# Transition matrices of a WKV scan: two heads worked half a level apart, projection products in pairs, VectorE's other work cut into pieces

## The reference

```python
def step(state, inp):
    r_t, w_t, k_t, v_t, a_t, b_t = inp
    sa = jnp.einsum('bhij,bhj->bhi', state, a_t)
    state = state * w_t[:, :, None, :] + sa[..., None] * b_t[:, :, None, :] + v_t[..., None] * k_t[:, :, None, :]
    return state, jnp.einsum('bhij,bhj->bhi', state, r_t)
```

## Time and profile before

| | |
|---|---|
| Time, median of 3 runs | 2726.47 us (2725.36 to 2730.03) |
| Time of the profiled execution | 2733.0 us |
| Span of the profiled execution | 2731.2 us |
| TensorE busy | 2640.0 us, 97% of the span |
| VectorE busy | 1676.8 us, 61% |
| ScalarE, GpSimd busy | 693.8 us, 25%; 317.5 us, 12% |
| Mean granted TensorE clock | 0.989 |

### The profile page before, as it was taken

One profiled execution on the slowest core, in us unless ns is written; L12 is line 12 of the kernel. 1 busy time (PEld: TensorE's weight loads), 2 busy tenths in 40 slices (PEclk: granted clock), 3 DMA queues, 4 the chain that ended last, 5 costly groups with the idle time before them and its releaser, 6 DMA issues.

```text
span 2731.2 us, 43464 instructions
## 1 busy us (share of the span) xinstructions
PE 2640.0 (97%) x17855; PEld 1986.6 (73%) x17855; DVE 1676.8 (61%) x2220; ACT 693.8 (25%) x1205; POOL 317.5 (12%) x277
## 2 busy tenths in 40 slices
PE   7999899999999999999999999989999999999998
PEld 3555456888878878888767777766677887788887
DVE  4888776555457665554476677754554665655554
ACT  4233433111010021110143344434420212201102
POOL 2000231000000010000123333332020100100001
PEclk8999899999999999999999999999999999999999
DMA  7575302333323323333311211113143333233332
GB/s 265 182 252 193 96 24 86 98 93 97 97 83 99 94 85 93 101 96 93 111 46 35 61 43 35 35 58 89 33 114 84 94 116 101 70 100 94 99 95 74
DMA packets 394851, 260.38 MB, mean 95 GB/s; under 512 B 19831, under 2 KB 376784, under 8 KB 394320
## 3 DMA queue, kind: packets, MB, share of 16 engines
q1 hardware_dynamic: 391456, 246.78, 30.4%
q0 software_dynamic: 2768, 9.83, 1.1%
q10 hardware_dynamic: 480, 1.64, 0.2%
HBM read 252.96 MB, written 4.46 MB: 94 GB/s over the span
## 4 chain that ended last, share of the span: by engine, by line
PE 87%; DVE 8%; ACT 2%; issue 2%; DMA 1%; SPq 0%; DVEq 0%; ACTq 0%
PE PS L902 13%; PE PS L904 13%; PE PS L903 13%; PE PS L1726 3%; PE PS L917 3%; PE PS L919 3%; PE PS L918 3%; PE PS L1728 2%; PE PS L1727 2%; DVE ARENA L2831 2%; PE PS L2062 2%; PE PS L2064 2%; PE PS L2063 2%; PE PS L1848 1%; PE PS L889 1%
## 5 line engine op out<-in xcount | busy, mean ns | idle before, releaser
L928 DVE CAST WH<-W 128x1024 fp32r<-128x1024 f32 x272 | 191.1, 703 | 353.6 <-PE PS L904 302.9
L930 DVE TENSOR_TENSOR WL<-W,WH 128x1024 fp32r<-128x1024 f32 x272 | 335.4, 1233 | 9.3
L903 PE MATMUL PS<-XNL,WH 128*128 128x512 f32 x832 | 323.7, 389 | 0.0
L902 PE MATMUL PS<-HH,WH 128*128 128x512 f32 x672 | 262.0, 390 | 0.2 <-DVE HL L3216 0.2
L904 PE MATMUL PS<-HH,WL 128*128 128x512 f32 x672 | 261.5, 389 | 0.0
L903 PE MATMUL PS<-HL,WH 128*128 128x512 f32 x672 | 261.4, 389 | 0.0
L902 PE MATMUL PS<-XNH,WH 128*128 128x512 f32 x512 | 199.3, 389 | 0.0
L904 PE MATMUL PS<-XNH,WL 128*128 128x512 f32 x512 | 199.2, 389 | 0.0
L903 PEld LDWEIGHTS PS<-XNL,WH 128*128 128x128 f32 x832 | 156.2, 188 | 33.0 <-issue 0.7
L917 PE MATMUL PS<-XNH,WH 128*128 128x512 f32 x384 | 151.1, 394 | 0.6 <-DVE XNL L848 0.5
L919 PE MATMUL PS<-XNH,WL 128*128 128x512 f32 x384 | 149.5, 389 | 0.0
(11 more groups left out here) (565 smaller groups left out, 5209.1 us busy)
## 6 DMA issues: line engine op xcount, KB each, us to landing
ARENA<-in_ada_w SPq DMA_DIRECT2D x80, 512.0 KB, 5.1
W<-in_ffn_w SPq DMA_DIRECT2D x64, 512.0 KB, 3.9
W<-in_w_in SPq DMA_DIRECT2D x51, 512.0 KB, 3.8
W<-in_ffn_w_gate SPq DMA_DIRECT2D x44, 512.0 KB, 3.7
W<-in_ffn_w_up SPq DMA_DIRECT2D x44, 512.0 KB, 3.6
W<-in_ffn_w_down SPq DMA_DIRECT2D x32, 512.0 KB, 3.7
W<-in_sc_w_in SPq DMA_DIRECT2D x24, 512.0 KB, 3.7
ARENA<-in_ada_w SPq DMA_DIRECT2D x8, 1024.0 KB, 18.0
```

The source lines that it names most:

```text
L902: nc.tensor.matmul(dst, WH[:, h, c], hi(k), start=(start and k == 0), stop=False)
L903: nc.tensor.matmul(dst, WH[:, h, c], lo(k), start=False, stop=False)
L928: nc.vector.tensor_copy(WH[:, h, 0:n], W[:, s, 0:n]).then_inc(parted, 1)
L930: nc.vector.tensor_tensor(WL[:, h, 0:n], W[:, s, 0:n], WH[:, h, 0:n], ALU.subtract).then_inc(freed[s], 1)
```

## The change: what it does

The two heads of a pair are no longer worked together in a step. TensorE's order in a level is now `p` of head 0, `xz` of head 1 *of the level before*, `xz` of head 0, `p` of head 1, and then one fill of two pieces of the projection in place of two lone fills. The fills begin behind level 2 and end in level 16 (in the last pass level 4 to level 32). The bonus product and head 1's `xz` of level 32 stand at the end, and `w` waits for each head's sum separately. ScalarE copies the projection's result (`raw1`) between the two heads' `pm` of level 2. VectorE's work for the next pair is cut into pieces, one behind each head's sum, and the reciprocal of 512 columns is done in three parts (176, 168, 168) in place of two. No product, sum or copy is added or dropped apart from that one reciprocal.

```diff
+        beside = {(0, 0): "d1", (0, 1): "m1 kkr", (1, 0): "d0", (1, 1): "m0", (2, 1): "nmax", (3, 0): "ninv0", (3, 1): "ninv1", (4, 0): "ninv", (4, 1): "nk"}
...
-                           + " ".join(f"p{l}0 p{l}1" + (next_pair("kss") if l == 2 else " bonus " if l == 4 else " ") + f"xz{l}0 xz{l}1"
-                                      for l in levels)
+                           + " ".join(f"p{l}0 " + (f"xz{l - 1}1 " if l else "") + f"xz{l}0" + next_pair("kss" if l == 2 else "") + f"p{l}1" for l in levels)
+                           + f" bonus xz{len(LEVELS) - 1}1 "
...
+                def masked(l, e):
+
+                    pe.wait_ge(p_pool.sem, p_pool.done(f"m{l}{e}", at))
+                    pe.wait_ge(p_dve.sem, p_dve.done(f"z{l - 1}{e}" if l else "xi", at))
+                    for t in range(NT):
+                        n = 4 * e + t
+                        for c, own in enumerate(halves):
+                            far = halves[1 - c]
+                            mm = nc.tensor.matmul(bank[e][own, t * CHUNK:(t + 1) * CHUNK], MT[far, n, :], XZ[far, e, 0, t, :], start=True, stop=True)
+                            if l == 1:
+                                mm = nc.tensor.matmul(bank[6][own, n * HEAD:(n + 1) * HEAD], GR[own, n, 2, :], TOK[own, t, 3, halves[e]], start=True, stop=True)
+                    mm.then_inc(p_pe.sem, p_pe.step(f"p{l}{e}"))
+
+                def both_sides(l, e):
+
+                    pe.wait_ge(p_act.sem, p_act.done(f"pm{l}{e}", at))
+                    pe.wait_ge(p_dve.sem, p_dve.done(f"z{l - 1}{e}" if l else "zi", at))
+                    for t in range(NT):
+                        n, cols = 4 * e + t, slice(t * CHUNK, (t + 1) * CHUNK)
+                        for c, own in enumerate(halves):
+                            if l < len(LEVELS) - 1:
+                                nc.tensor.matmul(bank[2 + 2 * e][halves[1 - c], cols], XZ[own, e, 1, t, :], PM[own, n, :], start=True, stop=True)
+                        for own in halves:
+                            mm = nc.tensor.matmul(bank[3 + 2 * e][own, cols], PM[own, n, :], XZ[own, e, 1, t, :], start=True, stop=True)
+                    mm.then_inc(p_pe.sem, p_pe.step(f"xz{l}{e}"))
+
                 for l in levels:
-                    for e in range(2):
-                        pe.wait_ge(p_pool.sem, p_pool.done(f"m{l}{e}", at))
-                        pe.wait_ge(p_dve.sem, p_dve.done(f"z{l - 1}{e}" if l else "xi", at))
-                        for t in range(NT):
-                            n = 4 * e + t
-                            for c, own in enumerate(halves):
-                                far = halves[1 - c]
-                                mm = nc.tensor.matmul(bank[e][own, t * CHUNK:(t + 1) * CHUNK], MT[far, n, :], XZ[far, e, 0, t, :], start=True, stop=True)
-                                if l == 1:
-                                    mm = nc.tensor.matmul(bank[6][own, n * HEAD:(n + 1) * HEAD], GR[own, n, 2, :], TOK[own, t, 3, halves[e]], start=True, stop=True)
-                        mm.then_inc(p_pe.sem, p_pe.step(f"p{l}{e}"))
-                    if l == 0 and ahead:
+                    masked(l, 0)
+                    if l:
+                        both_sides(l - 1, 1)
+                    elif ahead:
                         projection(1, range(5, KD), "raw0", "B", "lk")
-                    if l:
-                        early(range(2 * l - 2, 2 * l - 1))
+                    both_sides(l, 0)
                     if l == 2 and ahead:
                         pe.wait_ge(p_act.sem, p_act.done("ksq", at))
                         nc.tensor.matmul(bank[6], PAIR_ONES, YS, start=True, stop=True).then_inc(p_pe.sem, p_pe.step("kss"))
-                    if l == 4:
-                        pe.wait_ge(p_act.sem, p_act.done("kroot" if ahead else "akv", at))
-                        pe.wait_ge(p_dve.sem, p_dve.done("rk", at))
-                        nc.tensor.matmul(bank[6], PAIR_ONES, RK, start=True, stop=True).then_inc(p_pe.sem, p_pe.step("bonus"))
-                    for e in range(2):
-                        pe.wait_ge(p_act.sem, p_act.done(f"pm{l}{e}", at))
-                        pe.wait_ge(p_dve.sem, p_dve.done(f"z{l - 1}{e}" if l else "zi", at))
-                        for t in range(NT):
-                            n, cols = 4 * e + t, slice(t * CHUNK, (t + 1) * CHUNK)
-                            for c, own in enumerate(halves):
-                                if l < len(LEVELS) - 1:
-                                    nc.tensor.matmul(bank[2 + 2 * e][halves[1 - c], cols], XZ[own, e, 1, t, :], PM[own, n, :], start=True, stop=True)
-                            for own in halves:
-                                mm = nc.tensor.matmul(bank[3 + 2 * e][own, cols], PM[own, n, :], XZ[own, e, 1, t, :], start=True, stop=True)
-                        mm.then_inc(p_pe.sem, p_pe.step(f"xz{l}{e}"))
-                    if l:
-                        early(range(2 * l - 1, 2 * l))
+                    masked(l, 1)
+                    first = 2 * l if ahead else 2 * l - 2
+                    if 0 <= first < KD:
+                        early(range(first, first + 2))
+                pe.wait_ge(p_act.sem, p_act.done("kroot" if ahead else "akv", at))
+                pe.wait_ge(p_dve.sem, p_dve.done("rk", at))
+                nc.tensor.matmul(bank[6], PAIR_ONES, RK, start=True, stop=True).then_inc(p_pe.sem, p_pe.step("bonus"))
+                both_sides(len(LEVELS) - 1, 1)
                 pe.wait_ge(p_act.sem, p_act.done("akv", at))
-                pe.wait_ge(p_dve.sem, p_dve.done(f"z{len(LEVELS) - 1}1", at))
                 for n, (e, t) in enumerate(items):
+                    if t == 0:
+                        pe.wait_ge(p_dve.sem, p_dve.done(f"z{len(LEVELS) - 1}{e}", at))
...
+                        if l == 0 and e == 0 and ahead:
+                            raw("rw", 1, i, 7, p_act)
                     if l == 0 and ahead:
-                        raw("rw", 1, i, 7, p_act)
...
-            def key_norm_begun(at, p_act, p_dve):
+            def key_bound(at, p_act, p_dve):
 
                 dve.wait_ge(p_act.sem, p_act.done("kroot", at))
                 ts(RSTD[:, 0:T], ROOT[:, 0:T], 1e-12, None, ALU.max).then_inc(p_dve.sem, p_dve.step("nmax"))
-                dve.wait_ge(p_dve.sem, p_dve.done("nmax", at))
-                nc.vector.reciprocal(RSTD[:, 0:T // 2], RSTD[:, 0:T // 2]).then_inc(p_dve.sem, p_dve.step("ninv0"))
-
-            def key_norm(at, p_act, p_dve):
-
-                nc.vector.reciprocal(RSTD[:, T // 2:T], RSTD[:, T // 2:T]).then_inc(p_dve.sem, p_dve.step("ninv"))
+
+            def key_inverse(n, at, p_dve):
+
+                third = slice((0, 176, 344)[n], (176, 344, T)[n])
+                if n == 0:
+                    dve.wait_ge(p_dve.sem, p_dve.done("nmax", at))
+                nc.vector.reciprocal(RSTD[:, third], RSTD[:, third]).then_inc(p_dve.sem, p_dve.step(("ninv0", "ninv1", "ninv")[n]))
+
+            def key_normed(at, p_dve):
...
+            def beside_sums(l, e, pair, at, p_act, p_dve, signalled):
+
+                if (l, e) == (0, 0):
+                    if signalled:
+                        dve.wait_ge(go_dve.sem, signalled("out"))
+                    shifted(1, at, p_act, p_dve)
+                elif (l, e) == (0, 1):
+                    mixed_in(1, pair, at, p_dve)
+                    key_scaled(pair, at, p_dve)
+                elif (l, e) == (1, 0):
+                    shifted(0, at, p_act, p_dve)
+                elif (l, e) == (1, 1):
+                    mixed_in(0, pair, at, p_dve)
+                elif (l, e) == (2, 1):
+                    key_bound(at, p_act, p_dve)
+                elif (l, e) in ((3, 0), (3, 1), (4, 0)):
+                    key_inverse(2 * l + e - 6, at, p_dve)
+                elif (l, e) == (4, 1):
+                    key_normed(at, p_dve)
...
-                    if l == 0 and ahead:
-                        if ended:
-                            dve.wait_ge(go_dve.sem, signalled("out"))
-                        shift_mix(1, pair + 1, at, p_act, p_dve)
-                        key_scaled(pair + 1, at, p_dve)
-                    if l == 1 and ahead:
-                        shift_mix(0, pair + 1, at, p_act, p_dve)
-                    if l == 2 and ahead:
-                        key_norm_begun(at, p_act, p_dve)
-                    if l == 3 and ahead:
-                        key_norm(at, p_act, p_dve)
+                        if ahead:
+                            beside_sums(l, e, pair + 1, at, p_act, p_dve, signalled if ended else None)
                 if ahead:
```

More of the change, by code:

```diff
@@ L579, in two_blocks @@
         rf_pool = prog("rf_pool", "l1")
-        rf_dve = prog("rf_dve", "lr lk lv d0 m0 d1 m1 kkr cs t km d2 m2 nmax ninv0 ninv nk bb rt at0 at bt kt")
+        rf_dve = prog("rf_dve", "lr lk lv d0 m0 d1 m1 kkr cs t km d2 m2 nmax ninv0 ninv1 ninv nk bb rt at0 at bt kt")
```

(22 more changed lines are left out.)

## The result

The changed kernel takes 2737.09 us (median of 9 runs, 2734.87 to 2747.15); the kernel before, run beside it, 2728.31 (9 runs, 2724.7 to 2732.61). The ratio is 1.0036, with a 95% interval of 1.0025 to 1.0047: slower by 8.8 us. The forecast had 2732 and +5.6.

A forecast was written before the change was run, and what follows sets the result against it. TensorE was taken to bound the kernel, with one short wait a pass to win. Six steady passes +3.2, first +0.4, last +2.0 gave +5.6 us, 2732 on the median; range 2720 to 2738, the forecast's own 2728 to 2736.

The forecast's parts named there:

- 3.2+0.4+2.0: Extra us in all passes: six steady passes +3.2, the first about +0.4, the last +2.0; total +5.6.
- rival 3: Slower: more idle in each pass lowers TensorE's clock; 1.5 us a pass, +10.5 on the forecast, 2742; chance 0.08.
- The starting point: Whole run: forecast added +5.6 to the profiled execution's 2733.0, then took 6.5 off for the median: 2732.1, rounded to 2732.
- the 0.2 taken off for borders between small products: Four borders in levels 2 and 8: bounds 0 and 0.44 us, 0.2 taken, bringing a steady pass from +0.73 to +0.5.
- The chain of 1.69 us: One head's `xz`, sum, next `p`: 1.69 us, seen in level 2; makes head 1's `p` wait 0.59 in three levels.
- Rival 1: Faster: the wait at head 1's `p` is mostly hidden, 2717.6, or about 2725 half hidden; chance 0.18.
- Level 4: Steady pass, level 4, with 0.61 for `p`: 4.50 us against 4.11, +0.39.
- Level 8: Steady pass, level 8: key-norm product covers head 1's wait, 4.77 us against 4.81, -0.04.
- Six steady passes: The six steady passes were priced alike at +0.5 us each, +3.2 together.
- The last pass: No key-norm product, so levels 4, 8 and 16 all pay: +2.25 us, less borders +2.0.
- VectorE's pieces at nothing: VectorE's pieces behind each sum: bounds 0 and 0.3 us a pass, taken 0; tight place `m1` and `kkr` after level 2.
- the low clock stays: Last pass: 1.48 us of the old levels' time put down to low clock, expected to stay, leaving +2.25 before borders.

The follow-up runs named there:

- the double fill at level 8: lone-fill kernel with level 8's two fill pieces joined at the level's end, except in the last pass: 2723.73 us, ratio 0.9979; again 2723.79, 0.9983.
- the blocks: Changed kernel with VectorE's work for the next pair back in blocks behind a level's second sum: 2755.68 us, ratio 1.0085 to the kernel before.
- the double-fill run: Kernel before, heads still together, with both fill pieces behind `p` in levels 4 to 32 and none behind `xz`: 2747.76 us, ratio 1.0062.
- lone-fill kernel: Changed kernel with fill pieces apart again, one back between the two `xz`: 2723.57 us, ratio 0.9983 to the kernel before.

## Why the prediction was right and where it was off

- **The step that failed: all that lies outside the passes, and the granted clock over the whole run, was put at nothing.** The sum was 3.2+0.4+2.0 from the passes alone, and rival 3 priced a lower clock in the passes only. The passes gave +5.9 for +5.6, but the medians gave 8.8 and, the second time, 6.4. The three profiles of each kernel have +2.2 behind the passes and -0.9 ahead of them. Behind the passes the code is the same, and its time goes with the clock. Four profiles, all 3770 products from the end of the last pass to the end: the kernel before (first and third profile), the double fill at level 8 (second profile), and the blocks:

```profile
1864.22:2731.20 866.98, 839.97 (x3770) 667.12 (x3770) 484.46 (x609) 177.37 (x334) 60.35 (x38) 1.00 0.31 90
1856.92:2727.10 870.18, 843.83 (x3770) 670.08 (x3770) 483.35 (x609) 177.47 (x334) 60.44 (x38) 0.99 0.31 89
1855.00:2726.40 871.40, 844.78 (x3770) 669.87 (x3770) 483.81 (x609) 177.46 (x334) 60.31 (x38) 0.99 0.31 89
1882.99:2760.00 877.01, 849.59 (x3770) 673.93 (x3770) 484.29 (x609) 177.35 (x334) 59.84 (x38) 0.98 0.30 89
```

Over all thirteen profiles this part took 866.7 to 877.1 us, with 9.8 to 36.1 us of it at 1.2 GHz; a us more at 1.2 GHz goes with 0.39 us of time. The kernel before had 10.1, 16.5 and 20.8 us there, the changed one 20.2, 17.3 and 20.9: on average 3.7 more, by that slope 1.4 of the 2.2 us. A link to longer passes doesn't hold up: the third row's kernel has the shortest steady pass of all, 56.20 to 56.27. Why the changed kernel had the lower clock (0.9883 to 0.9899 over all runs, about 3 us by the table at the result) stays open.
- **The starting point**: the forecast stood on a median of 2726.5 over 3 runs, where 9 gave 2728.3: 1.8 of the 5 us by which it was too low.
- **A second step that failed: the 0.2 taken off for borders between small products.** The discount was taken off without a row that showed such a gain, and none came. The prices as they stood gave +0.73, against +0.83 measured over the levels and +0.94 over passes 3 to 6 (the usual pass alone, 57.55 to 56.70, +0.85). Over those four passes the discount is 0.8 of the 1.6 us by which they took longer than forecast.
- **What bounds the kernel**: right. What moved in the passes is on TensorE's path, and the waits are where the prediction put them: three a pass at head 1's `p` in levels 4, 16 and 32, none at head 0's `p` of level 4 but in the last pass, level 8 without one.
- **The chain of 1.69 us**: right in the main, though seen once a pass before. In level 16 the level's first product to head 1's `p` took 2.16 for 2.23, and the double-fill run has 1.69 to the hundredth. Rival 1, in which it would have been hidden, is out.
- **Level 4**: 4.29 for 4.50. Head 0's `p` took 0.52 (1589.37 to 1589.89), where I had 0.61, and the chain from there to head 1's `p` 1.56, where I had 1.69. **Level 8**: 5.05 for 4.77, spread over three joints. Head 1's `p` of level 4, then rows of level 8:

```profile
1591.45 0.24 PE L1848 MATMUL PS<-ARENA 64*64 64x64 f32 x1 [0.18 <-DVE ARENA L3413]
...
1593.66 0.62 PE L1848 MATMUL PS<-ARENA 64*64 64x64 f32 x14
...
1594.82 0.14 PEld L1861 LDWEIGHTS PS<-ARENA 64*64 64x64 f32 x2 [0.15 <-ACT ARENA L2601]
...
1596.50 0.68 PE L1848 MATMUL PS<-ARENA 64*64 64x64 f32 x16
```

Head 0's `xz` began 1.16 after head 0's `p` (priced 1.09), as it had to wait for its copy. It and the key-norm product took 1.68 (1.55), and `p` and the double fill 2.21 to the next level's start at 1598.71 (2.13).
- **Six steady passes**: I took them as alike. Passes 2 and 7 lost nothing, for the stalls told above, so six gave +3.65 and not 6 x 0.94. The forecast's 3.2 is near by luck: a discount that never came against stalls that went.
- **The last pass**: +1.63 for +2.0. The old wait stayed as forecast:

```profile
1821.65 0.33 PE L1848 MATMUL PS<-ARENA 64*64 64x64 f32 x1 [2.40 <-DVE ARENA L3413]
```

In this profile its levels took 21.23 against 20.19, +1.04 for +2.25 before the discount. Levels 8 and 16 took 4.27 each and level 32 with `w` 7.49, near the 4.36 and 7.74 of the sum, against 3.95, 3.95 and 6.70 before. Level 4 took 5.20 against 5.59: there the sum added a wait to a stretch at low clock, as if the clock slowed the waiting too. The three profiles of the changed kernel differ by the clock; in the second the levels had 0.87 in place of 0.93:

```profile
1823.73:1846.13 22.40, 21.64 (x474) 17.42 (x474) 6.24 (x10) 4.56 (x11) 6.74 (x7) 0.87 0.10 26
```

The third had 21.40 at 0.92, and the kernel before 20.10 to 20.19 at 0.92 in all three. So the levels account for +1.52 of the +1.63. By what a us at 1.2 GHz costs in the last section, I estimate some 0.3 of it as clock and the rest as the order.
- **VectorE's pieces at nothing**: right as far as the waits show. The tight place is behind head 1's sum of level 2:

```profile
1591.22 0.74 DVE L3288 SCALAR_TENSOR_TENSOR ARENA<-ARENA,COLS 128x512 f32<-128x512 f32 x1
1592.12 0.48 DVE L3292 TENSOR_SCALAR ARENA<-ARENA,COLS 128x512 f32<-128x512 f32 x1 [0.15 <-DVE ARENA L3288]
1592.52 0.68 DVE L3413 TENSOR_TENSOR ARENA<-ARENA,PS 128x512 f32<-128x512 f32 x1
```

The two pieces took 1.3 instead of 1.79, and the sum with its release was done at 1593.36, 0.3 ahead of `p` at 1593.66.
- **The clock in the passes** (rival 3): the steady pass kept 1.00, with three short waits for sums and one of 0.8. In the last pass "the low clock stays" holds only in part. Both kernels stand idle for 3.6 us ahead of that pass's level 2, and the low clock first comes about the end of that wait (it ends at 1818.29 before and at 1815.61 after), not behind the 2.3 to 2.4 us wait. In the kernel before it comes in two stretches (the first two rows) with 1.00 between them, over the 2.3 us wait; in the changed one it lasts through that wait (the third row):

```profile
1818.66:1822.07 3.41, 3.29 (x91) 2.95 (x86) 3.37 (x3) 0.77 (x2) 2.88 (x3) 0.50 0.02 5
1825.49:1828.90 3.41, 3.41 (x70) 2.56 (x67) 0.69 (x1) 0.87 (x2) 0.94 (x2) 0.50 0.00 0
1814.52:1824.75 10.23, 6.13 (x168) 5.68 (x172) 7.78 (x9) 2.21 (x4) 4.71 (x5) 0.50 0.01 2
```

The Trainium skill (TensorE: Matmul & The Clock Gate, "HAM oscillation — how this bites in real kernels") describes a kernel whose clock falls because its short bursts of work stand between waits for DMA. The fall at the 3.6 us wait agrees with it; by the 1.00 of the steady pass the new waits are too short.
- **The total**: that the passes came out at +5.9 for +5.6 is luck in part. The discount and the lost stalls cancel, and so in part do the 0.4 too much in the last pass and the 0.2 too little in the first.

## What to carry to other kernels

A piece of independent work is worth what it covers, not what its border costs. Before two fillers are joined to save borders (0.11 us each here), list the chains that each covers; a chain longer than what is left beside it (1.69 against 1.10) shows up whole. An order that staggers two heads and keeps each filler apart gained 0.17% (0.17 to 0.21% with one pair joined where a product covers the chain), where staggering with all fillers joined lost 0.25 to 0.36%. Take no discount off a sum for which no row speaks. And before a forecast of some us in 2700, look at how far runs of one kernel spread with the granted clock: here 1.9 us for each 0.001.

## What the runs showed of the chip

- Idle in the rows under-reads a stall. A wait printed as 0.30 made a stretch 0.5 to 0.6 longer than its work, since the ends of products are modelled; starts are the better ruler.
- A low clock cost time here where it fell on work, and none where TensorE waited for another engine. The lone-fill kernel and the one with a double fill at level 8 run the same code in the last pass, and differ by 2 us; the first of these rows is the lone-fill kernel's, the second the other's:

```profile
1797.77:1852.24 54.47, 46.81 (x991) 35.15 (x989) 26.78 (x38) 15.55 (x31) 16.85 (x16) 0.91 0.20 60
1799.38:1851.81 52.43, 44.58 (x991) 33.52 (x990) 26.79 (x38) 15.55 (x31) 16.86 (x16) 0.97 0.21 63
```

Up to `p` of level 4, through two waits for VectorE, they take 14.48 and 14.46 us at clocks of 0.81 and 0.88. From head 1's `p` of level 4 on they take 35.48 and 35.41. The whole difference lies between, where one has 0.50 and the other 1.00 for the same products:

```profile
1812.25:1816.76 4.51, 4.51 (x103) 3.65 (x107) 0.69 (x1) 0.80 (x2) 0.73 (x1) 0.50 0.01 4
1813.84:1816.40 2.56, 2.56 (x103) 2.09 (x107) 0.69 (x1) 0.80 (x2) 0.73 (x1) 1.00 0.02 6
```

That is 1.95 us for 4.51 at 1.2 GHz, 0.43 for each. The second profile of the latter kernel had 0.93 over the pass and still took 52.42 us: its low clock ended at 1816.56, ahead of this stretch. Its first part took 14.47 us at 0.76. What makes the low clock last longer in one run than in another was not found.
